# Places of an expert's rows dealt over the DMA engines, and the third pair looked up with the first two

## The chip, the cores and the metric

The kernel runs on one core of a Trainium2 chip. The metric is device microseconds (us) from the start to the end of the execution; lower is better. Three runs of the kernel before took 950.89, 952.76 and 957.0 us.

## The reference, cut to what matters

Two layers of an encoder over 256 prompt tokens and 128 sample tokens, 384 in all, width 1024. Layer 0 mixes by attention and retention, layer 1 by a convolution module. Behind each stands the mixture of experts that the change touches, over all 384 tokens:

```python
grp = jnp.argmax(g_logits, axis=-1)                 # 1 of 4 groups
e_sel = take_along_axis(e_logits, grp)[:, 0]        # its 8 experts
top_v, top_i = lax.top_k(e_sel, TOP_K)              # 2 of the 8
top_w = jax.nn.softmax(top_v, axis=-1) * p_grp
...
a = jnp.einsum('nd,edf->nef', x, w_gate[g])
u = jnp.einsum('nd,edf->nef', x, w_up[g])
hid = jax.nn.silu(a) * u * gates[:, g, :, None]
out = out + jnp.einsum('nef,efd->nd', hid, w_down[g])
```

Every token goes to 2 of 32 experts, so there are 768 rows of work for 32 experts in each layer. All is float32. An expert's weights are 3 MB, so a layer has 96 MB of them.

## The kernel before

**Places.** The experts are worked through in 16 pairs. A pair has a tile of 128 partitions: 64 places (`CAP`) for each of its two experts, expert `e` in partitions 64e to 64e + 63. A token's rank among the tokens of its expert (`SV`, counted from 0) is its place. If an expert had more than 64 tokens, the whole loop over pairs would run again for the next 64 (a window); `extra_windows` finds on VectorE how many windows are needed, by comparing the fullest expert's count with 64, 128 and so on, and writes it to `steps` (semaphore `steps_known`), which all engines read. Here one window is run in each layer.

**Lookup.** For a pair, VectorE builds one-hots (`onehot`, line 1843; `first_onehots`, line 1797, for the first two pairs): `G[token, expert of the pair, place] = (iota[place] == SV)`. TensorE multiplies them with a table `TB` of four columns per token and expert (destination row, source row, 1/rms, gate) in `looked_up`, line 1009: 12 small matmuls into PSUM bank 6 or 7. VectorE turns the result into `IDX` (row numbers) and `SC` (scales) in `index_out`, line 1849. An empty place gets row number 1024, which is beyond the bounds of the indirect DMA and moves nothing. `G` has two buffers, `G[:, p % 2]`.

**Rows.** GpSimd gathers the rows of pair p by `IDX` from the tensor `rows` in HBM into `XGT[:, p % 2]` (`gather`, line 560), and scatters the pair's results from `Y` into `outs` (`scatter`, line 567). Pair 0 is not gathered: TensorE picks its rows by a product with `G` (`first_rows`, line 994). The last pair is not scattered: its `Y` is added to `X` through products with its transposed one-hots `GT` (`combined`, line 1102).

**TensorE's order in the loop over pairs** (line 1131 on): first half of gate/up of pair p (line 1058, 16 matmuls), second half, transposes of the gathered rows of p + 1 (line 1035), lookup of p + 2 (line 1023), down product of p - 1 (line 1081), transposes of the hidden activations (line 1067). In pair 0 the lookups of pairs 0 and 1 stand between the two halves. VectorE's order (line 1904 on): for pair 0 and 1 `index_out`, then one-hots of pair 2, and in each pair `hidden`, `rows_out` (line 1870, the transposed rows to `XG`), `index_out` of p + 2 and one-hots of p + 3. GpSimd issues the gather of p + 2 as soon as its `IDX` is written and the buffer is free.

**Weights.** The expert weights come as 1 MB loads of 128 partitions, six to a pair (four gate/up, two down), issued by SyncE into a ring of 18 slots (`expert_load`, line 408). A load is issued when the product that read its slot has ended (`freed`). Behind the last loads of layer 0 come loads of the convolution's weights (`w_pw1`); at the end of a layer SyncE reads `outs` back (line 422), and VectorE adds it to `X` (helper line 1535).

Of the kernel before, what the change touches and what calls it, by code (L numbers as in the profile page):

```python
# [20 lines left out]
ALU = mybir.AluOpType  # L21
# [62 lines left out]
def layout(parts):  # L84
# [8 lines left out]
    ("ident", P), ("tri", P), ("strict", P), ("ones", P), ("blk", P), ("mask", 2 * P), ("smask", TOK), ("suffix", P), ("cos", NT * 32), ("sin", NT * 32), ("iota", CAP), ("tie", EPG),  # L93
# [18 lines left out]
def constants():  # L112
# [24 lines left out]
    put("iota", np.broadcast_to(np.arange(CAP), (P, CAP)))  # L137
# [59 lines left out]
def build(nc, a, o):  # L197

    with ExitStack() as ctx:
# [130 lines left out]
        GT = rm("GT", [P, TOK])  # L330
# [278 lines left out]
        def _(pe):  # L609
# [378 lines left out]
            def moe(lay, extra0):  # L988
# [20 lines left out]
                def looked_up(b, u, p, unit, cols):  # L1009

                    n = len(range(4)[cols])
                    pe.wait_ge(S("g_ready"), b + (2 * lay + p + 1))
                    if unit < 0:
                        pe.wait_ge(S("code_ready"), lay + 1)
                        pe.wait_ge(S("tb_ready"), lay + 1)
                    elif unit == 0:
                        pe.wait_ge(S("gates_ready"), lay + 1)
                    elif unit == NP:
                        pe.wait_ge(S("gt_ready"), u + 1)
                    past(pe, "idx_read", u * UNITS + (lay + (1 + max(unit - 1, 0) if unit >= 0 else 0)))  # L1020
                    for t in range(NT):
                        for e in range(2):
                            last = mm(PS[CAP * e:CAP * (e + 1), 6 + unit % 2, 0:n], G[:, p % 2, 2 * t + e, :],
                                      TB[:, t, 2 * (p % NP) + e, cols], start=t == 0, stop=t == NT - 1, skip_group_check=True)
                    last.then_inc(S("idx_done"), 1)
# [45 lines left out]
                def down(b, u, p):  # L1071

                    pe.wait_ge(S("hidT_ready"), b + (p + 1))
                    if p:
                        pe.wait_ge(S("y_ready"), b + p)
                    full_pair(u, 6 * p + 4)
# [51 lines left out]
                with pe.Fori(0, n + 1) as w:  # L1128
                    b, u = b0 + w * NP, u0 + w
                    for p in range(NP):  # L1130
                        gate_up(b, u, p, 0)
                        if p == 0:
                            looked_up(b, u, 0, 0, slice(0, 4))
                            looked_up(b, u, 1, 1, slice(0, 4, 3))
                        elif p == NP - 1:
                            down(b, u, p - 1)
# [3 lines left out]
                        looked_up(b, u, p + 2, p + 2, slice(0, 4) if p + 2 < NP else slice(1, 3))  # L1140
# [389 lines left out]
        def _(dve):  # L1530
# [265 lines left out]

            def first_onehots(p, t0, t1, sem=None):

                q.do(V.tensor_tensor(G[:, p, 2 * t0:2 * t1, :], bc(C["iota"], 1, 2 * (t1 - t0)),
                                     bc(SV[:, p, 2 * t0:2 * t1], 2, CAP), ALU.is_equal), sem)  # L1800
# [39 lines left out]
            def moe(lay, extra0):  # L1840
                gain = 2 * lay + 1

                def onehot(u, p):

                    dve.wait_ge(S("idx_done"), u * UNITS + (lay + p))
                    V.tensor_tensor(G[:, p % 2, :, :], bc(C["iota"], 1, NT * 2), bc(SV[:, p % NP, :], 2, CAP),
                                    ALU.is_equal).then_inc(S("g_ready"), 1)

                def index_out(u, p, unit, kinds, cols):
# [3 lines left out]
                    V.tensor_scalar(IDX[:, p % NP, kinds], PS[:, 6 + unit % 2, 0:n], float(EMPTY), None, ALU.add)  # L1853
                    V.tensor_copy(SC[:, p % NP, cols], PS[:, 6 + unit % 2, n:2 * n]).then_inc(S("idx_read"), 1)  # L1854
# [32 lines left out]
                def extra_windows():  # L1887
# [3 lines left out]
                    ts(R8[:, 34:39], C["iota"][:, 1:MAXWIN], float(CAP), None, ALU.mult)  # L1891
                    ts(R8[:, 34:39], R8[:, 34:39], R8[:, 33:34], None, ALU.is_lt)
# [10 lines left out]
                with dve.Fori(0, n + 1) as w:  # L1903
                    b, u = b0 + w * NP, u0 + w
                    index_out(u, 0, 0, slice(0, 2), slice(0, 2))
                    index_out(u, 1, 1, slice(0, 1), slice(1, 2))
                    onehot(u, 2)
                    for p in range(NP):
# [3 lines left out]
                        if p + 2 < NP:  # L1912
                            index_out(u, p + 2, p + 2, slice(0, 2), slice(0, 2))
                        else:
# [181 lines left out]
```

## Time and profile before

| | |
|---|---|
| median of 3 runs | 952.76 us (950.89 to 957.0) |
| the profiled execution | 954.99 us, span of its instructions 953.2 us |
| PE (TensorE) | busy 865.0 us, 91% |
| DVE (VectorE) | busy 338.4 us, 35% |
| ACT (ScalarE) | busy 213.3 us, 22% |
| POOL (GpSimd) | busy 89.3 us, 9% |
| queue q1 (SyncE's loads and stores) | 36048 packets, 245.95 MB, 63.9% of 16 engines' span |
| queue q0 (GpSimd's, gathers and scatters among them) | 13328 packets, 30.02 MB, 9.0% |
| mean granted TensorE clock | 0.973 |

The share of busy time is over the whole span. The chain is the work that ended last, followed back from the end. In a table of windows each row is a stretch of the span, with the busy time of each engine (and the number of instructions), the granted clock of TensorE, the mean busy share of the 16 DMA engines, and what they moved in GB/s. In a timeline, `[2.27 <-DMA XGT<-rows,IDX]` says that the engine had been idle for 2.27 us and that this DMA ended the idle time; "issue" is idle time for which the profile shows no cause. Neighbouring instructions of one kind are merged into one row.

### The profile page before, as it was taken

To read this page: it belongs to the slowest core of one execution; us is meant where nothing else is said; L and a number is where in the kernel's file an instruction comes from. 1 tells how busy PE (TensorE), PEld (TensorE's weight loads), DVE (VectorE), ACT (ScalarE), POOL (GpSimd) and SP (SyncE) were. 2 spreads that over 40 slices of the span, in tenths; PEclk is the share of its full clock that TensorE was granted. 3 is DMA by queue.
4 is the path that set the end of the run, shared out by engine and by line. 5 is a ranking of instruction groups with operands and counts; after the bars stand their busy time and mean duration, and the time that the engine had idled before them with its cause. 6 is when DMAs were issued, how large, how long until landed. Compare 5 with 4: busy or idle time off the path is not lost.

```text
span 953.2 us, 14019 instructions
## 1 busy us (share of the span) xinstructions
PE 865.0 (91%) x5380; PEld 504.5 (53%) x5380; DVE 338.4 (35%) x814; ACT 213.3 (22%) x464; POOL 89.3 (9%) x106
## 2 busy tenths in 40 slices
PE   6999999999899999788778999969988999978774
PEld 5888888788733333233235555438963333323231
DVE  0512563432621111011055789972251111101105
ACT  3323234422211111101122222244121111101010
POOL 1400000000011111101100000000001111111110
PEclk9999999999899999999988999999999999999998
DMA  9962720776699999999988222036449999999975
GB/s 341 410 255 94 186 93 1 281 302 245 243 366 415 419 418 418 419 419 420 391 361 345 89 89 89 13 105 238 159 166 382 414 418 417 418 418 419 419 322 201
DMA packets 49441, 276.86 MB, mean 290 GB/s; under 512 B 11016, under 2 KB 11168, under 8 KB 20632
## 3 DMA queue, kind: packets, MB, share of 16 engines
q1 hardware_dynamic: 36048, 245.95, 63.9%
q0 software_dynamic: 13328, 30.02, 9.0%
q8 instruction: 43, 0.70, 0.3%
q14 instruction: 22, 0.18, 0.1%
HBM read 267.59 MB, written 30.61 MB: 313 GB/s over the span
## 4 chain that ended last, share of the span: by engine, by line
PE 64%; DMA 13%; SPq 12%; DVE 6%; issue 2%; ACT 2%; DVEq 0%; ACTq 0%; POOLq 0%
PE PS L1058 12%; PE PS L636 12%; SPq L408 12%; DMA slot<-in_experts 9%; PE PS L1176 8%; PE PS L889 7%; PE PS L1081 6%; DMA XGT<-rows,IDX 3%; PE PS L866 2%; PE PS L1035 2%; PE PS L1195 2%; DVE X L1535 2%; PE PS L994 1%; PE PS L1102 1%; DVE YC L1998 1%
## 5 line engine op out<-in xcount | busy, mean ns | idle before, releaser
L1058 PE MATMUL PS<-slot,XG 128*64 128x512 f32 x1024 | 236.5, 610 | 34.1 <-DMA slot<-in_experts 31.9
L1058 PEld LDWEIGHTS PS<-slot,XG 128*64 128x64 f32 x1024 | 74.6, 140 | 171.8 <-issue 167.1
L1861 DVE SCALAR_TENSOR_TENSOR hid_by_token<-PS,SC,SG 128x256 f32<-128x256 f32 x32 | 15.5, 484 | 360.5 <-ACT SG L1431 360.5
L636 PE MATMUL PS<-slot,HT 128*128 128x256 f32 x576 | 132.6, 386 | 7.7 <-ACT HT L1271 7.6
L1081 PE MATMUL PS<-slot,HID 128*64 128x512 f32 x512 | 118.2, 604 | 6.6 <-DMA slot<-in_experts 5.6
L636 PEld LDWEIGHTS PS<-slot,HT 128*128 128x128 f32 x576 | 108.6, 192 | 24.7 <-ACT HT L1271 8.3
L1176 PE MATMUL PS<-HC,slot 128*128 128x384 f32 x256 | 86.0, 491 | 1.6 <-DVE HC L1947 1.6
L1445 ACT ACTIVATE Y<-PS,SC 128x1024 f32<-128x1024 f32 x32 | 35.6, 1113 | 161.7 <-PE PS L1081 144.5
L1081 PEld LDWEIGHTS PS<-slot,HID 128*64 128x64 f32 x512 | 36.2, 138 | 64.1 <-issue 62.7
L1176 PEld LDWEIGHTS PS<-HC,slot 128*128 128x128 f32 x256 | 47.6, 190 | 40.2 <-issue 9.7
L1431 ACT ACTIVATE SG<-PS,SC 128x256 f32<-128x256 f32 x32 | 15.2, 474 | 232.8 <-PE PS L1058 232.8
L564 POOL DMA_INDIRECT XGT<-rows,IDX x34 | 34.7, 1020 | 310.8 <-DVE SC L1854 180.7
L1870 DVE TENSOR_TENSOR XG<-PS,small 128x512 f32<-128x512 f32 x68 | 43.5, 682 | 15.0 <-PE PS L1035 14.8
L889 PE MATMUL PS<-slot,YC 128*128 128x256 f32 x192 | 43.9, 390 | 3.0 <-ACT YC L1524 3.0
L1998 DVE SCALAR_TENSOR_TENSOR YC<-U,small,YC 128x384 f32<-128x384 f32 x74 | 45.2, 611 | 0.0
L1035 PEld LDWEIGHTS PS<-cst,XGT 128*128 128x128 f32 x256 | 27.4, 141 | 32.2 <-issue 25.0
L889 PEld LDWEIGHTS PS<-slot,YC 128*128 128x128 f32 x192 | 37.3, 196 | 8.9 <-issue 3.6
L1035 PE MATMUL PS<-cst,XGT 128*128 128x128 f32 x256 | 34.9, 279 | 6.0 <-DMA XGT<-rows,IDX 6.0
L1998 DVE SCALAR_TENSOR_TENSOR YD<-U,small,YD 128x384 f32<-128x384 f32 x66 | 40.3, 611 | 0.0
L572 POOL DMA_INDIRECT outs<-Y,IDX x30 | 30.2, 1007 | 102.1 <-ACT Y L1445 98.4
L1288 ACT ACTIVATE PJ<-PS,norms 128x256 f32<-128x256 f32 x36 | 16.9, 473 | 77.9 <-PE PS L636 77.5
L1195 PE MATMUL PS<-U,DG 32*32 32x384 f32 x736 | 22.5, 505 | 3.1 <-ACT stat L1492 3.1
(300 smaller groups left out, 820.2 us busy)
## 6 DMA issues: line engine op xcount, KB each, us to landing
slot<-in_experts SPq DMA_DIRECT2D x192, 1024.0 KB, 17.0
slot<-in_w_pw SPq DMA_DIRECT2D x12, 1024.0 KB, 10.2
slot<-in_w_in SPq DMA_DIRECT2D x11, 1024.0 KB, 11.5
outs<-slot POOLq DMA_DIRECT2D x12, 512.0 KB, 9.5
slot<-outs SPq DMA_DIRECT2D x6, 1024.0 KB, 7.6
slot<-in_w_out SPq DMA_DIRECT2D x4, 1024.0 KB, 7.4
rows<-X POOLq DMA_DIRECT2D x6, 512.0 KB, 8.7
KTC<-in_k_past POOLq DMA_DIRECT2D x1, 2048.0 KB, 13.6
```

The lines of the kernel that those rows point to most:

```text
L408: sp.dma_start(slot[RINGS[lay][place(q)]][:, :], experts[bass.ds(half * HALF + (lay * LOADS + q), 1), :, :].rearrange("o p n -> p (o n)")) ...
L564: pool.indirect_dma_start(XGT[:, p % 2, :], None, rows[lay], bass.IndirectOffsetOnAxis(IDX[:, p % NP, 1:2], 0), bounds_check=TOK - 1, oob_ ...
L636: last = mm(PS[:, in_bank(n), 0:UCOL], HT[:, k, P * t:P * (t + 1)], w[:, k, :], start=k == 0, stop=k == KD - 1)
L889: last = mm(PS[:, RING[i % 4], UCOL * (u % 2):UCOL * (u % 2) + UCOL], lhs[:, k, P * t:P * (t + 1)], w[:, k, :], start=k == 0, stop=k == ks ...
L1035: last = nc.tensor.transpose(PS[:, k // 4, P * (k % 4):P * (k % 4 + 1)], XGT[:, p % 2, P * k:P * (k + 1)], ident)
L1058: last = mm(PS[CAP * e:CAP * (e + 1), 2 + p % 2, :], XG[:, p % 2, k, CAP * e:CAP * (e + 1)], w[:, 2 * FE * (k % 4):2 * FE * (k % 4 + 1)], ...
L1081: last = mm(PS[CAP * e:CAP * (e + 1), 4 + n, :], HID[:, p % 2, j, e, :], w[:, j, 512 * n:512 * (n + 1)], start=j == 0, stop=j == 1, skip_g ...
L1176: last = mm(PS[:, 2 * (c % 2) + g, 0:TOK], w[:, k, P * cc:P * (cc + 1)], HC[:, k, :], start=k == 0, stop=k == KD - 1)
L1195: last = mm(PS[STRIP * j:STRIP * (j + 1), 4 + i, 0:TOK], DG[rows, c % 2, w, :], U[rows, c, :, w:w + LS], start=m == 0, stop=m == ROUNDS[c] ...
L1445: A(Y[:, p % 2, :], PS[:, 4:6, :].rearrange("p a n -> p (a n)"), ACT.Copy, scale=SC[:, p, 1:2]).then_inc(S("y_ready"), 1)
L1870: V.tensor_tensor(XG[:, p % 2, 4 * h:4 * h + 4, :], PS[:, h, :].rearrange("p (k n) -> p k n", n=P), bc(GC[:, gain, 4 * h:4 * h + 4], 2, P) ...
L1998: ins = V.scalar_tensor_tensor(acc, src, tap, acc, ALU.mult, ALU.add)
```

## The change

Three things. The constant `iota` becomes two tables of 64 ranks, one for even and one for odd pairs, so that a place no longer holds the rank of its own number. Place 0 to 3 of the first 32 hold ranks 0, 8, 16, 24, place 4 to 7 ranks 1, 9, 17, 25, and so on; odd pairs deal in the reverse order. The window thresholds get a table of their own, `wins`. And pair 2 gets its one-hots in a buffer `GA`, its lookup right behind those of pairs 0 and 1 and into PSUM bank 4, and its `index_out` before the first `hidden`.

```diff
-    ("cos", NT * 32), ("sin", NT * 32), ("iota", CAP), ("tie", EPG),
+    ("cos", NT * 32), ("sin", NT * 32), ("iota", 2 * CAP), ("wins", MAXWIN - 1), ("tie", EPG),
...
-    put("iota", np.broadcast_to(np.arange(CAP), (P, CAP)))
+    place_of = np.arange(CAP)
+    group, lane, row = place_of // 32, place_of // 4 % 8, place_of % 4
+    ranks = [32 * group + 8 * row + order for order in (lane, 7 - lane)]
+    put("iota", np.broadcast_to(np.concatenate(ranks), (P, 2 * CAP)))
+    put("wins", np.broadcast_to(CAP * np.arange(1, MAXWIN), (P, MAXWIN - 1)))
...
-        GT = rm("GT", [P, TOK])
+        GT = Region(rm.n, top_at)("GT", [P, TOK])
+        GA = rm("GA", [P, NT * 2, CAP])
+        def onehots(p):
+            return GA[:, :, :] if p == 2 else G[:, p % 2, :, :]
...                looked_up
+                    bank = 4 if unit == 2 else 6 + unit % 2
...
-                            last = mm(PS[CAP * e:CAP * (e + 1), 6 + unit % 2, 0:n], G[:, p % 2, 2 * t + e, :],
+                            last = mm(PS[CAP * e:CAP * (e + 1), bank, 0:n], onehots(p)[:, 2 * t + e, :],
...                down
                     if p:
                         pe.wait_ge(S("y_ready"), b + p)
+                    else:
+                        pe.wait_ge(S("idx_read"), u * UNITS + (lay + 4))
...                TensorE's loop over pairs
                             looked_up(b, u, 1, 1, slice(0, 4, 3))
+                            looked_up(b, u, 2, 2, slice(0, 4))
...
-                        looked_up(b, u, p + 2, p + 2, slice(0, 4) if p + 2 < NP else slice(1, 3))
+                        if p:
+                            looked_up(b, u, p + 2, p + 2, slice(0, 4) if p + 2 < NP else slice(1, 3))
...                VectorE
+            def ranks_of(p):
+                return C["iota"][:, CAP * (p % 2):CAP * (p % 2 + 1)]
...
-                    dve.wait_ge(S("idx_done"), u * UNITS + (lay + p))
-                    V.tensor_tensor(G[:, p % 2, :, :], bc(C["iota"], 1, NT * 2), bc(SV[:, p % NP, :], 2, CAP),
+                    dve.wait_ge(S("idx_done"), u * UNITS + (lay + (p if p > 2 else 1)))
+                    V.tensor_tensor(onehots(p), bc(ranks_of(p), 1, NT * 2), bc(SV[:, p % NP, :], 2, CAP),
...
-                    ts(R8[:, 34:39], C["iota"][:, 1:MAXWIN], float(CAP), None, ALU.mult)
-                    ts(R8[:, 34:39], R8[:, 34:39], R8[:, 33:34], None, ALU.is_lt)
+                    ts(R8[:, 34:39], C["wins"], R8[:, 33:34], None, ALU.is_lt)
...
+                    onehot(u, 2)
                     index_out(u, 0, 0, slice(0, 2), slice(0, 2))
                     index_out(u, 1, 1, slice(0, 1), slice(1, 2))
-                    onehot(u, 2)
+                    index_out(u, 2, 2, slice(0, 2), slice(0, 2))
```

TensorE at the start of the loop over pairs, in the kernel before. The lookups (`PS<-TB,G`) of pairs 0 and 1 are followed by the second half of gate/up of pair 0 (`slot_62`, `slot_63`, eight rows, the last of which is shown), the transposes of pair 1's rows, and then the lookup of pair 2.

```order
L1023 MATMUL PS<-TB,G 64x4 x6
L1012 REGISTER_ALU
L1023 MATMUL PS<-TB,G 64x2 x6
L1054 REGISTER_ALU
...
L1058 MATMUL PS<-slot_63,XG 64x512
L1031 ISA
L1035 MATMUL PS<-cst,XGT 128x128 x8
L1012 REGISTER_ALU
L365 REGISTER_ALU
L1023 MATMUL PS<-TB,G 64x4 x6
L1067 MATMUL PS<-cst,hid_by_token 128x128 x2
```

The same place in the changed kernel:

```order
L1034 MATMUL PS<-TB,G 64x4 x6
L1023 REGISTER_ALU
L1034 MATMUL PS<-TB,G 64x2 x6
L1023 REGISTER_ALU
L1034 MATMUL PS<-TB,GA 64x4 x6
L1065 REGISTER_ALU
...
L1069 MATMUL PS<-slot_63,XG 64x512
L1042 ISA
L1046 MATMUL PS<-cst,XGT 128x128 x8
L1078 MATMUL PS<-cst,hid_by_token 128x128 x2
```

The lookup of pair 2 moved from behind the transposes of pair 1 to ahead of the second half of gate/up of pair 0. Each such row stands for the two experts of three token tiles.

VectorE at the start of the same loop before, from the first `index_out` in it to that of pair 2 (`L1870` is `rows_out` of pair 1, `L1846` the one-hots):

```order
L1853 TENSOR_SCALAR IDX<-PS 128x2 [waits idx_done]
L1854 COPY SC<-PS 128x2
L1851 REGISTER_ALU
L1853 TENSOR_SCALAR IDX<-PS 128x1 [waits idx_done]
L1854 COPY SC<-PS 128x1
L1846 TENSOR_TENSOR G<-cst,SV 128x384 [waits idx_done]
L1858 ISA
L1861 SCALAR_TENSOR_TENSOR hid_by_token<-PS,SC,SG 128x256 [waits silu_ready]
...
L1870 TENSOR_TENSOR XG<-PS,small 128x512 [waits rows_tr]
L1851 REGISTER_ALU
L1853 TENSOR_SCALAR IDX<-PS 128x2 [waits idx_done]
```

And in the changed kernel:

```order
L1865 TENSOR_TENSOR GA<-cst,SV 128x384 [waits idx_done]
L1870 REGISTER_ALU
L1873 TENSOR_SCALAR IDX<-PS 128x2 [waits idx_done]
L1874 COPY SC<-PS 128x2
...
L1873 TENSOR_SCALAR IDX<-PS 128x1 [waits idx_done]
L1874 COPY SC<-PS 128x1
L1870 REGISTER_ALU
L1873 TENSOR_SCALAR IDX<-PS 128x2 [waits idx_done]
L1874 COPY SC<-PS 128x2
L1878 ISA
L1881 SCALAR_TENSOR_TENSOR hid_by_token<-PS,SC,SG 128x256 [waits silu_ready]
```

The one-hots of pair 2 moved ahead of both `index_out`, and the `index_out` of pair 2 moved ahead of the first `hidden`.

## Rows read from the trace of the kernel before

**Rows 1.** Chain that ended last, in order: start us, us, what.

```profile
308.53 7.02 PE PS L1058 x32
...
320.87 7.02 PE PS L1058 x32
...
446.62 28.94 DMA slot<-in_experts
...
895.88 29.54 DMA slot<-in_experts
```

**Rows 2.** Windows: busy us by engine, then clock, DMA share, GB/s; ordinary stretches.

```profile
280.00:290.00 10.00, 10.00 (x48) 3.28 (x48) 1.03 (x4) 1.39 (x2) 2.00 (x2) 1.00 0.99 410
...
730.00:740.00 10.00, 10.00 (x44) 3.17 (x42) 0.00 (x0) 1.39 (x2) 1.76 (x2) 0.91 0.91 359
...
840.00:860.00 20.00, 15.83 (x78) 5.74 (x74) 2.28 (x6) 1.86 (x3) 2.02 (x2) 0.91 1.02 419
```

**Rows 3.** Windows, the last 25 us of layer 1's weights.

```profile
905.00:910.00 5.00, 4.30 (x34) 2.16 (x31) 1.49 (x3) 0.48 (x1) 0.00 (x0) 1.00 1.02 425
910.00:915.00 5.00, 4.02 (x18) 1.48 (x19) 0.79 (x4) 1.21 (x2) 1.00 (x1) 1.00 0.98 406
915.00:920.00 5.00, 3.69 (x18) 1.30 (x19) 0.00 (x0) 0.18 (x1) 1.00 (x1) 1.00 0.83 338
920.00:925.00 5.00, 3.62 (x16) 1.20 (x16) 0.00 (x0) 1.11 (x1) 0.00 (x0) 1.00 0.60 247
925.00:930.20 5.20, 3.95 (x28) 1.85 (x28) 0.31 (x1) 0.47 (x1) 0.98 (x1) 1.00 0.42 169
```

**Rows 4.** Windows, the end of layer 0's weights.

```profile
467.00:470.00 3.00, 1.62 (x9) 0.40 (x6) 0.00 (x0) 0.00 (x0) 0.00 (x0) 1.00 0.94 369
470.00:475.00 5.00, 3.33 (x16) 1.04 (x12) 0.00 (x0) 1.11 (x1) 0.00 (x0) 1.00 0.84 352
475.00:480.00 5.00, 4.31 (x13) 1.63 (x15) 0.00 (x0) 0.00 (x0) 0.99 (x1) 0.66 0.75 315
480.00:484.30 4.30, 2.91 (x26) 1.43 (x24) 0.61 (x3) 0.86 (x2) 1.03 (x1) 1.00 0.58 242
```

**Rows 5.** Timeline, layer 1's end: start us, us, engine, line, operation [idle <-releaser].

```profile
915.00 3.65 PE L1058 MATMUL PS<-slot,XG 128*64 128x512 f32 x16 [0.96 <-DMA slot<-in_experts]
...
925.56 3.65 PE L1058 MATMUL PS<-slot,XG 128*64 128x512 f32 x16 [1.94 <-DMA slot<-in_experts]
...
942.53 7.52 DVE L1535 TENSOR_TENSOR X<-X,slot 128x1024 f32<-128x1024 f32 x6
```

**Rows 6.** Timeline, layer 0, first two pairs.

```profile
263.04 0.82 PE L1023 MATMUL PS<-TB,G 128*64 128x4 f32 x24
...
263.25 21.07 SPq L408 DMA_DIRECT2D slot<-in_experts  x10
263.55 0.16 DVE L1853 TENSOR_SCALAR IDX<-PS 128x2 int32<-128x2 f32 x1 [1.85 <-PE PS L1023]
...
263.71 3.64 PE L1058 MATMUL PS<-slot,XG 128*64 128x512 f32 x16
...
264.04 0.55 DVE L1846 TENSOR_TENSOR G<-cst,SV 128x384 f32<-128x384 f32 x1
...
268.30 0.52 PE L1023 MATMUL PS<-TB,G 128*64 128x4 f32 x12
...
270.68 1.01 POOL L564 DMA_INDIRECT XGT<-rows,IDX  x1 [8.91 <-DVE SC L1854]
...
278.47 1.07 PE L1035 MATMUL PS<-cst,XGT 128*128 128x128 f32 x8 [2.27 <-DMA XGT<-rows,IDX]
```

**Rows 7.** Timeline, layer 1, the wait for the third pair.

```profile
726.79 1.09 PE L1035 MATMUL PS<-cst,XGT 128*128 128x128 f32 x8 [3.25 <-DMA XGT<-rows,IDX]
```

**Rows 8.** Timeline, the first step of the window thresholds on VectorE.

```profile
257.38 0.17 DVE L1539 TENSOR_SCALAR R<-cst 128x5 f32<-128x5 f32 x1
```

**Rows 9.** DMA issues: out<-in, queue, count, KB each, median us to landing.

```profile
cst<-in_cst SPq DMA_DIRECT2D x1, 918.0 KB, 13.1
```

## Prediction: what binds, what the change costs and gives, and the number

> **What bounds the kernel now.** I read four views, in this order. The chain of waits first: it shows what the two mixtures of experts wait for. In the first half of a layer PE's own work is the chain: two neighbouring pairs' gate/up products start at 308.53 and 320.87, so a pair costs PE 12.34 us. In the second half the chain runs through the loads of expert weights, and each layer ends on one that took 29 us from issue to landing (446.62 + 28.94 = 475.56; 895.88 + 29.54 = 925.42) [rows 1]. A pair is six loads of 1 MB, 6.29 MB, and at 419 GB/s that is 15.0 us, without gathers and scatters: more than 12.34. So a layer ends when its DMA stream ends.
>
> The table of windows second, for what limits that stream. In full flow it shows a DMA share of 1.02 (all 16 engines busy; the records round up) at 419 GB/s [rows 2]. In layer 1's last 20 us the share falls 0.98, 0.83, 0.60, 0.42 and the rate with it: 406, 338, 247, 169 GB/s [rows 3]. Rate divided by share is 414, 407, 412, 402, against 417 at 905 to 910. So each engine moves its own 26 GB/s whether its neighbours work or not: the limit is the single engine, and the stream ends when the engine with most bytes is through. That it thins out over 20 us instead of ending at once says that the engines have unequal work. The last two loads are behind the one that the chain waits for: 2 x 1.049 MB / 418 GB/s = 5.0 us, and 925.4 + 5.0 = 930.4, where the share ends. Layer 0 thins out alike, 0.94, 0.84, 0.75, 0.58 to 484.3 [rows 4]; there four loads follow the one waited for (two of w_pw1), 10 us.
>
> **Part 1, the dealt ranks.** The weights (128 partitions, 8 KB each) are the same for all engines; only rows gathered and scattered can be unequal. An expert gets 768/32 = 24 tokens on average for 64 places and empty places move nothing, so places 0 to 23 of each half of a tile hold rows of 4 KB and 24 to 63 hold few.
> What evening them out is worth, from rows: idle engine time of the thinning, with 1.02 as full. Layer 1: 5 x (1 - 0.98/1.02) + 5 x (1 - 0.83/1.02) + 5 x (1 - 0.60/1.02) + 5.2 x (1 - 0.42/1.02) = 0.2 + 0.9 + 2.1 + 3.1 = 6.3 us [rows 3]. Layer 0: 0.2 + 0.9 + 1.3 + 1.9 = 4.3 us [rows 4]. With equal work all engines would end that much before the slowest does now, and the load waited for lands as much earlier.
> A second estimate, by counting: the diff deals by lane = place//4 modulo 8, each half of the tile apart. Taking these 16 groups as the 16 engines (no row names an engine) and counting the rows of each from the reference's own router on its inputs: in layer 0 the fullest engine carries 126 rows (15 gathers and 15 scatters), the mean is 90; in layer 1, where one expert has 44 tokens, 140 against 89. A row is 4096 B / 26.1 GB/s = 0.157 us, so the fullest is 5.7 and 8.0 us behind the mean. With the dealt ranks the fullest has 95 and 96: 0.8 and 1.1 us behind. By the count the change gives 4.9 + 6.9 = 11.8 us; by the shares, less the same remainder, 3.5 + 5.2 = 8.7. The count is an upper value (it has the last scatter in it, which the waited-for load is not behind), the shares a lower one (light engines' idle time is partly filled by what is issued late). I take the middle, 10.2 us.
> The Trainium skill (DMA: Bandwidth & Descriptors, section The descriptor swizzle) gives the same groups, four neighbouring partitions to an engine, repeated after 32, the upper 64 on the other eight. The trace's thinning in steps agrees with it but doesn't prove it.
> Can PE follow? In the last pairs each of its steps waits for a load (0.96 us before gate/up of pair 15 at 915.00, 1.94 at 925.56) [rows 5], and it needs 12.34 us a pair where DMA needs over 15. So yes. What follows the last load is dependent work, 925.56 to 953.2 in layer 1, and moves as one: the output rows are added back from 942.53 without a wait on their load [rows 5].
>
> **Part 2, the third pair's lookup moved forward.** Now: one-hots of pair 2 built at 264.04 (0.55 us), looked up by 12 matmuls at 268.30 (0.52 us) behind the transposes of pair 1, gather issued at 270.68, and PE waits 2.27 us for it at 278.47 [rows 6]; in layer 1 it waits 3.25 us at 726.79 [rows 7]. After: the lookup stands right behind the first 24 matmuls at 263.04, so the gather can start near 265.4, over 5 us earlier, and both waits go (2.27 and 3.25 are less than 5). But PE's pace is not the bound of the layer: a wait of PE costs only where it leaves DMA without a freed slot. In layer 1 the share falls to 0.91 at 730 to 740: 10 x (1 - 0.91/1.02) = 1.1 us [rows 2]. In layer 0 the share of 0.99 at 280 to 290 is 0.3 us, a part of it ordinary; I take 0.1. Gain 1.2 us of the 5.5 that PE stops waiting.
> Its costs: the 12 matmuls now stand inside gate/up of pair 0 and free the next two slots 0.5 us later. The two slots that the first half frees are reloaded from 263.25 on; these loads last 5.0 us, to 268.3, and the next slots, freed now at 263.71 + 3.64 = 267.4, come at 267.9 [rows 6]: hidden; without that cover 0.5 us a layer. VectorE's one-hots of pair 2 come first in the loop, ahead of two small copies (idle 1.85 us there now, row at 263.55 [rows 6]); 0.55 fits. If they are late, PE waits at most that 0.55. The move changes no DMA count: same gathers, one is earlier in POOL's queue, directly behind gather 1, with nothing between.
> Bank 4 for this lookup makes the first down product wait for its reading, which is over two gate/up halves earlier: nothing. GA's bytes lie under GT, written eleven pairs later: nothing.
>
> **Part 3, small ones.** The window thresholds come from a table, so one linked VectorE step goes (0.17 us at 257.38 and its link, 0.2 us [rows 8]); it stands ahead of the step that fills XG for PE's first gate/up. That is 0.2 us a layer, 0.4, if PE's row products don't end later anyway; I take 0.3. The constants grow by 69 columns x 512 B = 35 KB on 918 KB [rows 9]: 0.1 us at that load's rate, under PE's first products: nothing.
>
> **Sum.** 10.2 + 1.2 + 0.3 = 11.7 us. The profiled execution took 954.99 us around its span of 953.2; 954.99 - 11.7 = 943.3. The median of the three runs is 2.2 lower, so 941.1 against 952.76.
>
> **Rivals.**
> *The limit is shared after all.* If HBM or the fabric set 419 GB/s, equal queues would end the stream at the same total, and only part 2 and 3 stay: 952.76 - 1.5 = 951.3. For it: 419 stands like a wall for 200 us. Against it: rate over share stays at 402 to 417 with less than half of the engines busy [rows 3]. The Trainium skill (DMA: Bandwidth & Descriptors, Where 436 GB/s comes from) has about 358 GB/s per core as the HBM side's limit, which would bind first; the trace shows 419, so it doesn't hold here. Chance 0.06.
> *The engines that have least now are slow ones.* Engines given less work can't show that they are slow; with a full share they would finish last, and the gain of part 1 goes the more the slower they are. If they would need all of the slack that they now have, 951.3. Against it: the share already falls in 910 to 915 [rows 3], so the lightest are done 15 to 20 us before the end, about what (140 - 26) x 0.157 = 18 us by the count allows at equal speed. The Trainium skill (same page, Latency and other measured facts) says that engines 7 and 15 are usually slower; by the groups above these are the lightest now (26 rows), so it speaks against this change. Chance 0.08.
> *Half the gain.* Something else takes over before the stream ends as early: the chain of down product, scatter and slot reuse, or PE, whose waits in the last pairs are only 1 to 2 us each [rows 5]. Part 1 gives 5 us: 952.76 - 6.5 = 946.3. Chance 0.19.
> *Slower.* Dealt ranks make the four places of an engine point to rows that are eight ranks apart. If row reads from HBM then took twice the time, 90 rows x 0.157 = 14 us a layer on each engine would come on top: 952.76 + 28 - 12 = 969. It decides from 40% on. Against it: a row is one 4 KB piece either way, and tokens of one expert are scattered rows already. Chance 0.03.
> *Forecast.* 0.64.
>
> **Numbers.** One per cent of 952.76 is 9.5 us, about what a measurement of this kernel can tell from no change (its three runs spread 6 us). Part 1's bounds of 8.7 and 11.8 give a total of 10.2 to 13.3, both beyond it; with the spread of runs, 0.57 of the forecast's 0.64 is faster by over 1%, and 0.03 of the half gain: 0.60 faster. Slower by over 1%: 0.03 + 0.01 for a stall that I don't see: 0.04. The rest, 0.36, within 1%. The likeliest case's own range is 938 to 944; the range 937 to 949.5 takes in the half gain and leaves out the two cases of no gain, the slower one and some spread.
>
> **What would show it.** Right: a share of 1.01 to 1.02 until some 6 us before the last expert load's end and then a fall within 3 us; the last waited-for load lands near 471 in layer 0 and near 914 in layer 1; gather 2 issued near 265.4, no PE wait in front of the third pair's transposes. Wrong on part 1: the thinning is as long as now, or a steady share below 1. Wrong on part 2: PE waits inside gate/up of pair 0, or a new dip of the share near 265 to 275. A lower rate over share than 402 to 417 would mean slower rows. The prediction fails first on the middle between 8.7 and 11.8, which no row decides.

## The result, and the profile after

| | before | changed |
|---|---|---|
| median, 6 runs each | 954.71 us (950.89 to 957.0) | 946.62 us (945.18 to 948.83) |
| ratio to before, 95% interval | | 0.992 (0.9893 to 0.9947) |
| span of the profiled execution | 953.2 us | 943.4 us |
| last waited-for expert load lands, layer 0 | 475.56 us | 471.61 us |
| last gate/up starts, layer 1 | 925.56 us | 915.76 us |

By that ratio the changed kernel is faster by 7.6 us (5.1 to 10.2). Two more timings of the same file on other occasions gave 0.9912 (0.988 to 0.9945) and 0.9901 (0.987 to 0.9932), 8.4 and 9.4 us. The mean of the three is 8.5 us; 11.7 were forecast.

The first views are the page's head lines of the changed kernel:

```profile
span 943.4 us, 14021 instructions
PE 863.8 (92%) x5380; PEld 502.9 (53%) x5380; DVE 338.1 (36%) x812; ACT 213.4 (23%) x464; POOL 89.4 (9%) x106
q0 software_dynamic: 13328, 30.02, 9.2%
```

Same work, same packets, a shorter span: next to nothing was removed, it only ends earlier. (Two VectorE instructions fewer are the threshold steps.)

The table of windows of the changed kernel at the end of layer 0's stream and of layer 1's (busy us by engine, clock, DMA share, GB/s), to be read against [rows 3, 4]:

```profile
467.00:472.00 5.00, 3.19 (x16) 1.09 (x14) 0.00 (x0) 1.11 (x1) 0.00 (x0) 1.00 1.01 420
472.00:477.00 5.00, 4.08 (x30) 1.81 (x26) 0.62 (x3) 0.47 (x1) 0.99 (x1) 1.00 1.01 418
477.00:481.00 4.00, 3.53 (x17) 1.06 (x16) 0.00 (x0) 0.38 (x1) 1.03 (x1) 1.00 0.68 273
...
905.00:910.00 5.00, 3.65 (x16) 1.26 (x16) 0.00 (x0) 1.07 (x2) 1.01 (x1) 1.00 1.02 415
910.00:915.00 5.00, 3.65 (x16) 1.26 (x16) 0.00 (x0) 1.09 (x1) 0.00 (x0) 1.00 1.01 418
915.00:920.00 5.00, 3.95 (x28) 1.84 (x28) 0.00 (x0) 0.44 (x2) 0.99 (x1) 1.00 0.61 244
```

All engines stay busy until 915 and then stop within 5 us, where before the share fell over 20 us. By the same sum as in the prediction the idle engine time at the end (the area that the share leaves below 1.02) is 4 x (1 - 0.68/1.02) = 1.3 us in layer 0 and 5 x (1 - 0.61/1.02) = 2.0 us in layer 1, where it was 4.3 and 6.3.

The timeline of the changed kernel in layer 0, against [rows 6], and its last gate/up product in layer 1, against [rows 5]:

```profile
262.35 0.56 DVE L1865 TENSOR_TENSOR GA<-cst,SV 128x384 f32<-128x384 f32 x1 [1.14 <-issue]
262.49 0.82 PE L1034 MATMUL PS<-TB,G 128*64 128x4 f32 x24
...
263.16 0.50 PE L1034 MATMUL PS<-TB,GA 128*64 128x4 f32 x12
...
264.82 1.01 POOL L574 DMA_INDIRECT XGT<-rows,IDX  x1 [3.55 <-DVE SC L1874]
...
275.94 1.09 PE L1046 MATMUL PS<-cst,XGT 128*128 128x128 f32 x8
...
719.53 1.09 PE L1046 MATMUL PS<-cst,XGT 128*128 128x128 f32 x8
...
915.76 3.65 PE L1069 MATMUL PS<-slot,XG 128*64 128x512 f32 x16 [1.96 <-DMA slot<-in_experts]
```

The third pair's one-hots are ready when PE comes to them, its gather starts at 264.82 instead of 270.68, and the transposes at 275.94 (layer 0) and 719.53 (layer 1) show no wait.

### The profile page after: what moved, and what is told of

Same layout as the page of the kernel before. It is cut to its first block, busy times and chain, and to the rows that moved or that the text cites. A ratio compares the mean times of both kernels' runs of the same rounds, so it can differ in the third digit from the quotient of the medians.

```text
span 943.4 us, 14021 instructions
## 1 busy us (share of the span) xinstructions
PE 863.8 (92%) x5380; PEld 502.9 (53%) x5380; DVE 338.1 (36%) x812; ACT 213.4 (23%) x464; POOL 89.4 (9%) x106
## 3 DMA queue, kind: packets, MB, share of 16 engines
q0 software_dynamic: 13328, 30.02, 9.2%
## 4 chain that ended last, share of the span: by engine, by line
PE 64%; SPq 16%; DMA 9%; DVE 6%; issue 2%; ACT 2%; DVEq 0%; ACTq 0%
SPq L418 16%; PE PS L1069 13%; PE PS L646 12%; PE PS L1191 9%; DMA slot<-in_experts 8%; PE PS L899 7%; PE PS L1094 6%; PE PS L876 2%; PE PS L1046 2%; PE PS L1210 2%; DVE X L1550 2%; PE PS L1004 1%; PE PS L1115 1%; PE PS L956 1%; DVE YC L2018 1%
## 5 line engine op out<-in xcount | busy, mean ns | idle before, releaser
L1881 DVE SCALAR_TENSOR_TENSOR hid_by_token<-PS,SC,SG 128x256 f32<-128x256 f32 x32 | 15.5, 484 | 355.3 <-ACT SG L1446 355.3
L1191 PEld LDWEIGHTS PS<-HC,slot 128*128 128x128 f32 x256 | 48.4, 193 | 41.0 <-issue 10.6
L1890 DVE TENSOR_TENSOR XG<-PS,small 128x512 f32<-128x512 f32 x68 | 43.5, 682 | 10.4 <-PE PS L1046 10.2
## 6 DMA issues: line engine op xcount, KB each, us to landing
slot<-in_experts SPq DMA_DIRECT2D x192, 1024.0 KB, 18.2
```

Source lines behind the costliest of these rows:

```text
L1191: last = mm(PS[:, 2 * (c % 2) + g, 0:TOK], w[:, k, P * cc:P * (cc + 1)], HC[:, k, :], start=k == 0, stop=k == KD - 1)
L1890: V.tensor_tensor(XG[:, p % 2, 4 * h:4 * h + 4, :], PS[:, h, :].rearrange("p (k n) -> p k n", n=P), bc(GC[:, gain, 4 * h:4 * h + 4], 2, P) ...
```

## The experiments

Theory A is the forecast's: each DMA engine has its own rate, and a layer ends when the fullest is through. Theory B: the limit is shared. Theory C: the engines that had least are slow. Theory D: what helps is the third pair's earlier gather. One measure is used throughout beside the timed ratio: **the layer's stretch**, from the start of its first gate/up product to the start of the last one that waits for a load, both from the profile's timeline. It leaves out what other stages do: between the two stretches lie 228 to 234 us, depending on the profile. The stretch has a spread of its own. Three profiles of the same changed file differ by 1.8 us in layer 0 and 0.6 in layer 1, so a single difference below that shows nothing.

| kernel | median us | ratio (95%) | layer 0: stretch | layer 1: stretch | counted lag us |
|---|---|---|---|---|---|
| before | 954.71 | 1 | 259.56 to 475.69: 216.1 | 706.83 to 925.56: 218.7 | 5.7, 8.0 |
| changed | 946.62 | 0.992 | 259.01 to 471.75: 212.7 | 702.43 to 915.76: 213.3 | 0.8, 1.1 |
| changed, c0 | 945.58 | 0.9912 | 259.48 to 471.01: 211.5 | 700.32 to 913.06: 212.7 | 0.8, 1.1 |
| changed, c1 | 945.22 | 0.9901 | 258.08 to 471.38: 213.3 | 700.66 to 913.87: 213.2 | 0.8, 1.1 |
| e1, deal only | 945.62 | 0.9908 (0.9875 to 0.9941) | 259.12 to 471.95: 212.8 | 702.58 to 916.38: 213.8 | 0.8, 1.1 |
| e2, third pair only | 952.94 | 0.9975 (0.9953 to 0.9997) | 256.93 to 472.99: 216.1 | 700.88 to 918.00: 217.1 | 5.7, 8.0 |
| e5, mirrored | 954.1 | 0.9991 (0.9967 to 1.0014) | 258.43 to 474.89: 216.5 | 707.99 to 925.44: 217.5 | 5.7, 8.0 |
| e6, one way | 947.12 | 0.9919 (0.9887 to 0.9951) | 257.83 to 471.84: 214.0 | 704.29 to 918.01: 213.7 | 2.3, 3.2 |
| e4, blocks | 972.79 | 1.0197 (1.0131 to 1.0264) | 259.30 to 483.89: 224.6 | 717.58 to 941.68: 224.1 | 16.2, 14.9 |
| e7, late gather | 959.82 | 1.0054 (1.0024 to 1.0084) | 259.06 to 479.72: 220.7 | 708.96 to 930.38: 221.4 | 0.8, 1.1 |
| e8, split | 946.11 | 0.9908 (0.9879 to 0.9937) | | | 0.8, 1.1 |
| e9, no rows | 918.48 | 0.9633 (0.9598 to 0.9669) | 257.85 to 457.54: 199.7 | 686.86 to 887.65: 200.8 | 0, 0 |
| e3, packed | 988.26 | 1.0358 (1.0284 to 1.0431) | 259.48 to 492.75: 233.3 | 723.44 to 956.51: 233.1 | 23.6, 23.7 |

The counted lag is (rows of the fullest group - mean) x 0.157 us, from the reference's router, as in the prediction. Each ratio is to runs of the kernel before on the same chip, whose medians were 954.86 (c0, e1, e2, e5), 954.59 (e3, e4, e6, e7) and 953.92 (c1, e8, e9).

### The two halves apart

> The change itself once more, beside its two halves on one chip. Theory A (fullest DMA engine ends the stream): 0.988 to 0.994 of the kernel before, and a last expert load that is waited for near 471.5 us in layer 0. Theory D (the gain is the third pair's earlier gather): the same total, but then the half without dealt ranks has it too.

> The change with the third pair's lookup, one-hots and read-out put back in their old places; dealt ranks and the threshold table stay. Theory A: part 1 measured in the profile of the change is 3.1 us in layer 0 and about 4.1 us in layer 1, so 7 to 8 us faster than before (0.992), PE's waits of 2.3 and 3.3 us ahead of the third pair's transposes back, and a share of about 0.91 in one 10 us stretch of layer 1. Theory B (shared limit) and theory D: 0.998 to 1.0.

```diff
                 looked_up, index_out
-                    bank = 4 if unit == 2 else 6 + unit % 2
+                    bank = 6 + unit % 2
                 TensorE's loop
-                            looked_up(b, u, 2, 2, slice(0, 4))
...
-                        if p:
+                        if True:
                             looked_up(b, u, p + 2, p + 2, slice(0, 4) if p + 2 < NP else slice(1, 3))
                 VectorE's loop
-                    onehot(u, 2)
                     index_out(u, 0, 0, slice(0, 2), slice(0, 2))
                     index_out(u, 1, 1, slice(0, 1), slice(1, 2))
-                    index_out(u, 2, 2, slice(0, 2), slice(0, 2))
+                    onehot(u, 2)
```

> The change with ranks in natural order, so that only the third pair's earlier lookup and the threshold table are left. Theory A: 1 to 2 us faster than before (0.998 to 1.0), no PE wait at the third pair, but a DMA share that thins out over some 17 us at the end of each layer as before. Theory D: 8 us faster (0.992).

```diff
-    ranks = [32 * group + 8 * row + order for order in (lane, 7 - lane)]
+    ranks = [place_of, place_of]
```

With the dealt ranks alone the ratio is 0.9908, the whole of the change's; with the third pair alone 0.9975. Theory D is out: it expected 0.992 of the latter. The profile of e1 has PE's waits for the third pair back (timeline, gathers and transposes in layer 0 and 1), and gains in spite of them:

```profile
270.24 1.01 POOL L574 DMA_INDIRECT XGT<-rows,IDX  x1 [8.87 <-DVE SC L1871]
277.21 1.06 PE L1046 MATMUL PS<-cst,XGT 128*128 128x128 f32 x8 [1.45 <-DMA XGT<-rows,IDX]
...
722.53 1.09 PE L1046 MATMUL PS<-cst,XGT 128*128 128x128 f32 x8 [3.24 <-DMA XGT<-rows,IDX]
```

In e2 the waits are gone and the stream thins out as before (windows of layer 1's end):

```profile
905.00:910.00 5.00, 4.05 (x21) 1.46 (x19) 0.00 (x0) 1.39 (x2) 1.00 (x1) 1.00 0.92 374
910.00:915.00 5.00, 3.66 (x19) 1.27 (x17) 0.00 (x0) 0.00 (x0) 0.00 (x0) 1.00 0.70 289
915.00:920.00 5.00, 3.05 (x14) 1.13 (x12) 0.00 (x0) 1.11 (x1) 0.99 (x1) 0.89 0.50 207
920.00:923.50 3.50, 3.50 (x23) 1.33 (x19) 0.00 (x0) 0.00 (x0) 0.00 (x0) 0.67 0.32 126
```

By stretches: dealing is worth 216.1 - 212.8 = 3.3 and 218.7 - 213.8 = 4.9 us without the third pair's move (before against e1), and with it, e2 against the mean of the three profiles of the change (212.5 and 213.1), 3.6 and 4.0: 7.6 to 8.2 us in all. The third pair's move is worth 0.3 + 0.7 = 1.0 us on top of dealing (e1 against that mean), 0.0 + 1.6 without it: no more than the spread of the stretch. The timed medians can't tell 1 us from nothing on top of dealing (945.62 against 945.58); without dealing, e2 is 2.4 us faster than before (0.3 to 4.5), the table of thresholds included.

### Are the lightly loaded engines slow?

> The change with ranks packed as in the kernel before but the eight lanes in reverse order: the engines that had least rows have most (136 and 140 rows of layer 1 on lane 7 of each half), the others mirrored. If all engines are equally fast (theory A): the same as with natural ranks, 0.998 to 1.0 of before, thinning over 17 us. Theory C (lane 7 of each half is a slow engine): longer than with natural ranks by what those engines lag; if they need their present slack of 114 rows x 0.157 us = 18 us, 18 us a layer, 1.035.

```diff
-    ranks = [32 * group + 8 * row + order for order in (lane, 7 - lane)]
+    ranks = [32 * group + 4 * (7 - lane) + row] * 2
```

The lanes that had the least rows now have the most. The end of layer 1 in its windows:

```profile
915.00:920.00 5.00, 3.66 (x18) 1.27 (x18) 0.00 (x0) 0.03 (x1) 1.00 (x1) 1.00 0.76 305
920.00:925.00 5.00, 3.49 (x16) 1.07 (x13) 0.00 (x0) 1.11 (x1) 0.00 (x0) 1.00 0.55 226
925.00:930.20 5.20, 3.95 (x28) 1.84 (x28) 0.43 (x2) 0.47 (x1) 0.99 (x1) 1.00 0.39 158
```

The stretches are 0.4 and 0.3 us longer than with natural ranks (e2), and the ratio is 0.9991 against 0.9975 with overlapping intervals. Theory C in its strong form (18 us a layer) is out. The 0.4 us is less than profiles of one file differ, so a lane that is slower by up to some 2 us in 217 is neither shown nor excluded. The Trainium skill (DMA: Bandwidth & Descriptors, section Latency and other measured facts) calls engines 7 and 15 usually slower; if the groups of places are the engines that the prediction took them for, no run here shows that.

### Making it worse, by count

> The change with ranks packed as tightly as the 16 groups allow: eight ranks to a group of places before the next group gets one. Counted on the reference's router, if the groups are places 4n to 4n + 3 and 32 + 4n to 32 + 4n + 3 of each half: the fullest group has 240 rows in either layer against a mean of 89, 23.6 and 23.7 us behind the mean, where natural ranks are 5.7 and 8.0 behind. Theory A with the full count: 33.6 us slower than natural ranks, about 985 us; with the two thirds of the count that the dealt ranks gave, 22 us, about 975. Rate over share in the tail stays near 410. Theory B: no change, 952. If the groups were eight neighbouring places, natural ranks would be as packed as these and the time would be that of natural ranks.

```diff
-    ranks = [32 * group + 8 * row + order for order in (lane, 7 - lane)]
+    ranks = [8 * lane + 4 * group + row] * 2
```

> The change with ranks dealt over eight blocks of eight neighbouring places (ranks 0, 8, 16 are places 0, 1, 2) instead of over lanes. With theory A's groups of four repeated after 32, only every other group gets rows: fullest 193 and 184, 16.2 and 14.9 us behind the mean, so 17.4 us slower than natural ranks by the full count, 970; 11 us by two thirds, 964. With groups of eight neighbours it would be as even as the change: 945.

```diff
-    ranks = [32 * group + 8 * row + order for order in (lane, 7 - lane)]
+    ranks = [8 * (place_of % 8) + place_of // 8] * 2
```

The timeline of e3 and then that of e4 (the starts of the stretches in layer 1, and the ends):

```profile
723.44 3.65 PE L1069 MATMUL PS<-slot,XG 128*64 128x512 f32 x16 [0.80 <-DVE XG L1890]
...
956.51 5.35 PE L1069 MATMUL PS<-slot,XG 128*64 128x512 f32 x16 [2.52 <-DMA slot<-in_experts]
```

```profile
717.58 3.65 PE L1069 MATMUL PS<-slot,XG 128*64 128x512 f32 x16 [0.88 <-DVE XG L1890]
...
941.68 3.65 PE L1069 MATMUL PS<-slot,XG 128*64 128x512 f32 x16 [2.53 <-DMA slot<-in_experts]
```

And the share in e3's windows:

```profile
900.00:920.00 20.00, 16.41 (x84) 6.26 (x82) 2.28 (x6) 1.86 (x3) 2.01 (x2) 0.95 1.01 403
...
940.00:950.00 10.00, 7.68 (x34) 2.72 (x34) 1.29 (x5) 1.39 (x2) 2.01 (x2) 1.00 0.40 163
950.00:960.00 10.00, 7.14 (x26) 2.70 (x28) 0.00 (x0) 1.11 (x1) 0.99 (x1) 0.84 0.29 118
```

With the same bytes, the same loads and the same instructions the two kernels are 33.7 and 18.2 us slower than before (954.59 beside them). Theory B expected no change and is out. Against natural ranks (e2) that is 35.3 and 19.9 us by the medians and 33.2 and 15.5 by the stretches, where the full count says 33.6 and 17.4. So the prices here are about the full count, not the two thirds that dealing had given: my second number in both expectations was wrong. The two also decide between the groupings that I had named. If an engine served eight neighbouring places, e4 would have been as even as e6 and e3 no worse than natural ranks. No row names an engine, but a count by four places, repeated after 32, comes within 2.5 us of both times. With less than half of the engines busy, rate over share is 163/0.40 = 408 and 118/0.29 = 407 GB/s: per busy engine that is the rate of the full stream (403/1.01 = 399), so an engine doesn't get faster when its neighbours rest.

### Making it a little worse

> The change with even and odd pairs dealt in the same direction. Fullest group by count 104 and 109 rows, 2.3 and 3.2 us behind the mean, where the change has 0.8 and 1.1: theory A expects 3.6 us more than the change by the full count (949), 2 to 3 by what the first runs gave. That is at the edge of what three rounds resolve; the share's thinning in the profile decides: 2 to 3 us of idle engine time at each layer's end against 0.5 to 1.9.

```diff
-    ranks = [32 * group + 8 * row + order for order in (lane, 7 - lane)]
+    ranks = [32 * group + 8 * row + lane] * 2
```

The windows of e6 at the end of layer 1:

```profile
910.00:915.00 5.00, 3.62 (x18) 1.26 (x16) 0.00 (x0) 0.00 (x0) 0.00 (x0) 1.00 1.02 418
915.00:920.00 5.00, 3.08 (x16) 1.09 (x14) 0.00 (x0) 1.11 (x1) 0.99 (x1) 1.00 0.71 290
920.00:922.50 2.50, 1.96 (x20) 0.93 (x16) 0.16 (x1) 0.47 (x1) 0.00 (x0) 1.00 0.43 169
```

Idle engine time here is 5 x (1 - 0.71/1.02) + 2.5 x (1 - 0.43/1.02) = 1.5 + 1.4 = 3.0 us, against 2.0 in the change; the stretches are 1.5 and 0.6 us longer than the mean of the change. The count said 1.5 and 2.1. The ratio, 0.9919, can't be told from the change's. So the profile agrees with a worth of about 2 us for reversing odd pairs, but its 1.5 us in layer 0 is inside the spread of the stretch.

### What PE's wait costs

> Dealt ranks with the third pair in its old place, and the gather of pair 2 made to wait until gate/up of pair 1 has ended, so that PE stands still about 8 us there in each layer instead of 2 to 3. If PE's wait is hidden as long as freed slots keep DMA busy (theory of part 2): two loads, 5 us, are covered, so 3 to 5 us a layer are lost, 6 to 10 in all, and the DMA share falls in 280 to 290 and 725 to 740. If a wait of PE always goes into the end: 12 us. If it never does, because PE catches up later: 0.

```diff
 (e1, and in gather on GpSimd)
+                if p == 2:
+                    pool.wait_ge(S("gu_done"), b * 2 + 4)
                 reached("idx_read", u * UNITS + (lay + 1 + (p + 1 if p >= 2 else 0)))
```

Timeline and windows of e7 in layer 0:

```profile
276.70 1.01 POOL L576 DMA_INDIRECT XGT<-rows,IDX  x1 [15.38 <-PE PS L1071]
284.88 1.94 PE L1048 MATMUL PS<-cst,XGT 128*128 128x128 f32 x8 [9.18 <-DMA XGT<-rows,IDX]
...
287.41 5.12 PE L1094 MATMUL PS<-slot,HID 128*64 128x512 f32 x16
```

```profile
280.00:285.00 5.00, 0.12 (x1) 0.15 (x2) 0.00 (x0) 0.00 (x0) 0.00 (x0) 0.52 1.01 422
285.00:290.00 5.00, 5.00 (x26) 2.83 (x28) 2.08 (x5) 0.00 (x0) 0.99 (x1) 0.50 0.18 74
290.00:295.00 5.00, 5.00 (x24) 1.63 (x22) 0.00 (x0) 1.39 (x2) 0.41 (x1) 0.96 0.37 105
```

The median was 959.82 us, 1.0054 (1.0024 to 1.0084) of before and 14 us over e1: 7 us a layer, by the stretches 7.8 and 7.6, for a wait of 9.18 us where e1 had 1.45, and 3 to 5 were expected. DMA is busy up to 285 with what had been issued and then dry, until the down product that the wait delayed frees its slots at 287.41 + 5.12 = 292.5. In e1 that product ends at 278.58 + 3.63 = 282.2, so its margin is 2.8 us, not the 5 that two loads last, and of the 10.3 us by which it is late 7.5 are over the margin: about the 7 to 7.8 measured. The clock adds to it: while PE stood still its granted clock fell to 0.52, about the lower of its two levels (1.2 of 2.4 GHz), and the transposes took 1.94 us instead of 1.06, the lookup 0.81 instead of 0.52 and the down product 5.12 instead of 3.63. That is 2.7 of the 10.3 us. The total alone wouldn't decide: the rival that every wait goes into the end says 12 us, the theory 6 to 10, and 14 came. The windows do decide for layer 0: DMA was still at its full share from 280 to 285 (1.01), the last 5 us of PE's wait. So the theory of part 2 holds in kind (what is under the cover costs nothing, what is over it costs in full), and two things in it were mis-sized: the cover is 2.8 us and not 5, and the slower clock behind the wait was left out.

### What the dealt ranks leave

> The change with 4096 instead of 1024 added to every row number, so that gathers and scatters are issued but no row is moved; the experts then work on rows that were never fetched. It asks what is left of the stream's unevenness with equal bytes on all engines. Theory A: the stream is 89 rows x 0.157 = 14 us shorter in each layer, 28 us in all (918), and all engines end within 1 us. If 1 to 2 us of idle engine time are left at the end of layer 1, the remainder that the dealt ranks leave is not the rows' doing but the engines' or the loads'. Rows may also have cost more than their own time: then more than 28 us.

```diff
-                    V.tensor_scalar(IDX[:, p % NP, kinds], PS[:, bank, 0:n], float(EMPTY), None, ALU.add)
+                    V.tensor_scalar(IDX[:, p % NP, kinds], PS[:, bank, 0:n], float(4 * EMPTY), None, ALU.add)
```

Its windows at the end of layer 1:

```profile
885.00:890.00 5.00, 3.60 (x18) 1.26 (x16) 0.00 (x0) 1.11 (x1) 0.99 (x1) 1.00 0.99 405
890.00:892.00 2.00, 1.60 (x19) 0.75 (x14) 0.01 (x1) 0.47 (x1) 0.00 (x0) 1.00 0.33 123
```

The median was 918.48 us, 26.7 less than the change beside it (945.22; 28 expected). The stretches are 257.85 to 457.54 = 199.7 us and 686.86 to 887.65 = 200.8 us, 12.8 and 12.3 less than the change's. The bytes of GpSimd's queue fell from 30.02 to 18.33 MB and its packets stayed 13328: 11.7 MB are the 2856 rows of 4096 B that the router's count gives for both layers, and at 419 GB/s they take 27.9 us. The idle engine time at the end, by the same sum, is 5 x (1 - 0.99/1.02) + 2 x (1 - 0.33/1.02) = 1.5 us with no row on any engine. So of the 2.0 us in the change 1.5 would be there with perfectly even bytes: the expectation's first case (within 1 us) fails, the second holds. The same sum for layer 0 gives 1.2 us (459 to 467), where the change has 1.3. The windows show no single engine; that 16 engines with equal loads end a little apart is the likeliest reading, and dealing can't win that.

> The change again, as the partner of the next two on one chip: 0.989 to 0.994 of the kernel before.

> The change plus one thing: in the last half gate/up product of each layer the eight matmuls of the first expert wait for that expert's load alone and run before those of the second. The load before the waited-for one lands 2.5 us earlier (1.049 MB at 419 GB/s) and PE stood idle 1.96 us there, so about 1.8 of the 3.65 us are done when the last load lands. If that load's landing is what ends each layer (theory A): 1.6 to 1.8 us a layer, 3.4 in all, 0.985 to 0.990 of the kernel before. If the down product's loads behind it take over: under 1 us a layer.

```diff
                 gate_up, last pair, second half; a semaphore of its own for the second expert's load
+                        full_pair(u, 6 * p + 2, both=False)
+                        for e in range(2):
+                            if e:
+                                full_last(u, 6 * p + 2)
+                            w = slot[RINGS[lay][place(6 * p + 2 + e)]]
+                            for k in range(4, KD):
...
```

Its timeline at that product in layer 0 (`PEld` is the weight load of a matmul), and behind it the same place in the change:

```profile
468.31 0.14 PEld L1080 LDWEIGHTS PS<-slot,XG 128*64 128x64 f32 x1 [0.26 <-DMA slot<-in_experts]
468.73 4.81 PE L1080 MATMUL PS<-slot,XG 128*64 128x512 f32 x13
...
470.45 0.14 PEld L1080 LDWEIGHTS PS<-slot,XG 128*64 128x64 f32 x1 [0.29 <-issue]
470.88 0.14 PEld L1080 LDWEIGHTS PS<-slot,XG 128*64 128x64 f32 x1 [0.29 <-issue]
...
471.18 0.27 PEld L1080 LDWEIGHTS PS<-slot,XG 128*64 128x64 f32 x3 [0.16 <-DMA slot<-in_experts]
...
474.24 0.59 PE L1080 MATMUL PS<-slot,XG 128*64 128x512 f32 x1
```

```profile
471.38 3.65 PE L1069 MATMUL PS<-slot,XG 128*64 128x512 f32 x16 [1.97 <-DMA slot<-in_experts]
471.83 0.17 PEld L1069 LDWEIGHTS PS<-slot,XG 128*64 128x64 f32 x2 [0.26 <-issue]
472.26 0.17 PEld L1069 LDWEIGHTS PS<-slot,XG 128*64 128x64 f32 x2 [0.26 <-issue]
```

This was the attempt to go beyond the change. The ratio was 0.9908 (0.9879 to 0.9937) against 0.9901 for the change beside it: nothing gained. From the first gate/up product to the last down product it took 257.68 to 476.96 = 219.3 us and 700.33 to 918.51 = 218.2 us, the change 258.08 to 477.16 = 219.1 and 700.66 to 919.65 = 219.0. At most 0.8 us of the 1.8 that I expected came, in layer 1 alone. The rows show why. In the change the matmuls of the two experts alternate, each uses 64 columns of the array (128*64 in the rows), and two of them start every 0.43 us: 16 take 3.65 us. In the split product one expert's matmuls stand alone, and only one starts every 0.43 us. So the eight matmuls of the second expert, begun when its load landed at 471.18, end at 474.24 + 0.59 = 474.83, 3.65 us later. That is as long as all sixteen take side by side. My step that half of the matmuls are half of the time was wrong: what ran early was work that had been free. So this run says nothing against the last load's landing as what ends a layer. No run with all its rows beat the changed kernel by more than the noise.

## Why the prediction was right, and where it was not

**What binds: right.** The stream of the fullest engine ends a layer. e3 and e4 move the end by 35.3 and 19.9 us (medians against natural ranks) by the places of the rows alone, and rate over share is 393 to 418 in the rows shown, with 5 or with 16 engines busy; the exceptions are the last 2 us of e9 (373) and the stretch in e7 where single loads start again (284). Whether the unit that limits is the engine itself or its path to its partitions these runs can't tell, since both follow the same places. The share's fall over 20 us was the right thing to look at.

**Part 1: right in kind, 10.2 us was too much.** By stretches it is 7.6 to 8.2 us (layer 0 3.3 to 3.6, layer 1 4.0 to 4.9); by the medians of e1 against before 8.8 us with an interval of 5.6 to 11.9. The term that was mis-sized is the middle between the two estimates. The idle shares' 8.7 was near and still 0.5 to 1.1 too much, the count's 11.8 was 3.6 to 4.2 too much; the reason that I gave for its being high, the last scatter, is at most a part. What was wrong in both is the remainder that I took from the count for the dealt ranks, 0.8 + 1.1 = 1.9 us. The profile of the change leaves 1.3 + 2.0 = 3.3 us idle, and e9 still leaves 1.2 + 1.5 = 2.7 with no rows at all. Of the 10.6 us idle before, 10.6 - 3.3 = 7.3 could so be won, and with perfect dealing 7.9. Taking the counted lag from the stretch leaves 209.4 us for e3's layer 1, 209.2 for e4's and 209.1 for e2's, but 212.0 for the change's (213.1 - 1.1). In layer 0 it leaves 209.7, 208.4 and 210.4, and 211.7 for the change. So from packed to natural ranks the time follows the count, within 0.3 us in layer 1 and 2.0 in layer 0, and from natural to dealt ranks it falls short by 1.3 to 2.9 us a layer. That even engines end apart by the 1.2 to 1.5 us of e9, which nobody sees while one of them is far behind the rest, is my reading. The remainder that the profile has over the count, 3.3 against 1.9, is 1.4 of the 3.6 to 4.2 us that are missing in all; the rest stays open.

**Part 2: right.** Gather 2 was forecast near 265.4 and started at 264.82; both waits are gone; the insertion of 12 matmuls and the one-hots cost PE no wait. 1.2 us were forecast; the stretches say 1.0 on top of dealing (1.6 without), which is within their spread, and the medians 2.4 (0.3 to 4.5) without dealing, part 3 included. So the size is not contradicted and not shown closely. That most of the 5.5 us of PE's wait is hidden was right; e7 shows that in layer 0 the margin beyond it is 2.8 us.

**Part 3:** 0.3 us; the first gate/up product of layer 0 starts at 259.01 against 259.56, but in other profiles of the same file at 259.48 and 258.08. Not resolved.

**The landings.** 471 in layer 0 was forecast, 471.6 came. 914 in layer 1 was forecast, and its last product started at 915.76. Layer 1 began 4.4 us earlier (702.43 against 706.83), about the 4.5 of the forecast's terms for layer 0. Its stretch is 5.4 us shorter, where the forecast's terms for layer 1 come to 7.3.

**The sum.** 11.7 us forecast, 7.6 (5.1 to 10.2) in the first timing, 8.5 in the mean of three. The median of the changed kernel, 946.6, lies in the range but outside the likeliest case's own 938 to 944. 2 us of that are the kernel before, whose median rose from 952.76 to 954.71 with more runs. The chance for faster by over 1% (0.60) was too high: a term of 8.7 would have put the sum at 10.2, close to the bound of 9.5, and the lower of two estimates deserved at least even odds.

**The rivals.** Shared limit: out (e3, e4). Slow engines: out beyond some 2 us a layer (e5). Slower rows in dealt order: out, since the change isn't slower and the rate over share in the full stream is 407 to 416, as before. Half the gain: nearest in its number, 946.3, but for another reason; neither PE nor the chain behind it took over, as the last product still waits for its load (1.96 us at 915.76).

## What to carry to other kernels

When tiles are sparsely filled and the DMA engines are the bound, look at how the busy share falls at the end of the stream: a long fall means that the places of the rows, not their number, set the time, and the integral of the idle share, less what even loads leave (1.2 to 1.5 us a layer here), is about what evening them out can give. Deal such rows over the engines (here groups of four partitions, repeated after 32, in each half of 128), since the same bytes cost from 945 to 988 us by their places alone. A wait of the computing engine in front of a saturated stream costs nothing up to the point where its delayed frees leave the queue empty, and everything beyond; in layer 0 here that was about 3 us. Two products that each fill half of the array's columns are best left alternating: pulling one ahead gains nothing (e8).

## What the runs showed that I had not expected

- The full count held for large unevenness (35.3 us for 33.6 counted, 19.9 for 17.4) but evening out the rest gave 1.3 to 2.9 us a layer less than the count.
- While PE waited for 9.18 us its granted clock fell to 0.52, its lower level, and it stayed low for the first product behind the wait: 16 matmuls took 5.12 us instead of 3.63. This wait so cost more than itself.
- With equal bytes on all engines and no rows (e9) a stream of 200 us still ended with 1.5 us of idle engine time.
- Rows out of bounds cost the stream nothing visible: with all of them so (e9), the 26.7 us saved are about the rows' own bytes (28).
- Matmuls of one expert alone start every 0.43 us, and those of two experts in turn, each on 64 columns, start two at a time (e8): 8 of the first take as long as 16 of the second.
